# Memory attention of a streaming encoder step: heads outside, tokens inside, turned to tokens outside, heads inside

## The reference

```python
def memory_block(x, mk, mv, norm_mem_q, w_mem_q, w_mem_o):
    bsz, L, _ = x.shape
    q = (rmsnorm(x, norm_mem_q) @ w_mem_q).reshape(bsz, L, MEM_HEADS, MEM_HEAD_DIM)
    s = jnp.einsum('bqhd,bkhd->bhqk', q, mk).astype(jnp.float32) * (MEM_HEAD_DIM ** -0.5)
    p = jax.nn.softmax(s, axis=-1).astype(mv.dtype)
    o = jnp.einsum('bhqk,bkhd->bqhd', p, mv).reshape(bsz, L, D_MODEL)
    return x + o @ w_mem_o
```

## Time and profile before

| | us |
|---|---|
| median of 3 runs | 1260.66 |
| lowest, highest run | 1258.69, 1265.19 |
| the profiled execution | 1260.04 |
| its span in the profile | 1258.3 |
| TensorE busy in the span | 1157.4 (92%) |
| VectorE, ScalarE busy | 721.6 (57%), 569.8 (45%) |
| mean granted clock of TensorE | 0.955 of full speed |

### The profile page before, as it was taken

How to read it: one execution, slowest core, us unless ns; L and a number is a source line. 1 busy time by engine, 2 the same in 40 slices (tenths; PEclk the granted TensorE clock), 3 DMA queues, 4 the chain that set the end, 5 groups by cost and what they waited for, 6 DMA issues and landing times.

```text
span 1258.3 us, 18236 instructions
## 1 busy us (share of the span) xinstructions
PE 1157.4 (92%) x7804; PEld 1040.9 (83%) x7813; DVE 721.6 (57%) x844; ACT 569.8 (45%) x705; POOL 118.1 (9%) x131
## 2 busy tenths in 40 slices
PE   5998897999969999999899989879949999999996
PEld 4997676999957799999899989559938877878884
DVE  4412774565168844233334733542479998898885
ACT  4423662333147652122213612521147776877873
POOL 1000441000025300000000000000010000000032
PEclk9998788999979999999899999979969999999998
DMA  9432000222220133233425622101179999999997
GB/s 280 134 110 67 1 1 4 81 70 83 59 60 2 34 84 90 63 93 93 142 87 200 201 83 68 34 1 51 67 283 385 412 420 395 380 401 400 353 317 180
DMA packets 95005, 197.24 MB, mean 157 GB/s; under 512 B 4185, under 2 KB 71929, under 8 KB 82633
## 3 DMA queue, kind: packets, MB, share of 16 engines
q1 hardware_dynamic: 87328, 169.88, 38.4%
q0 software_dynamic: 5408, 18.76, 5.1%
q10 hardware_dynamic: 2184, 7.39, 1.4%
HBM read 178.41 MB, written 17.60 MB: 156 GB/s over the span
## 4 chain that ended last, share of the span: by engine, by line
PE 72%; DVE 12%; ACT 9%; issue 3%; DMA 3%; POOL 0%; ACTq 0%; SPq 0%; DVEq 0%; POOLq 0%
PE ps L2022 45%; PE ps L924 7%; ACT buf_r L852 3%; DVE buf_r L859 3%; PE ps L934 3%; PE ps L2389 1%; PE ps L2140 1%; DMA buf<-in_w_gate_e 1%; ACT buf_r L434 1%; PE ps L2141 1%; DVE buf_r L1060 1%; DMA buf<-in_w_in 1%; PE ps L2111 1%; ACT buf_r L422 1%; PE ps L2258 1%
## 5 line engine op out<-in xcount | busy, mean ns | idle before, releaser
L2022 PE MATMUL ps<-buf_r,buf_r 128*128 128x288 f32 (+1 forms) x4560 | 598.8, 293 | 12.8 <-DVE buf_r L438 9.7
L2022 PEld LDWEIGHTS ps<-buf_r,buf_r 128*128 128x128 f32 x4560 | 592.5, 191 | 14.7 <-issue 5.9
L428 DVE TENSOR_TENSOR buf_r<-buf,buf_r 128x2048 fp32r<-128x2048 f32 (+2 forms) x53 | 116.6, 2200 | 175.7 <-ACT buf_r L422 175.7
L859 DVE TENSOR_TENSOR buf_r<-buf,buf_r 128x2048 fp32r<-128x2048 f32 x96 | 214.1, 2284 | 3.2 <-ACT buf_r L852 3.2
L924 PE MATMUL ps<-buf_r,buf_r 128*128 128x512 f32 x768 | 186.2, 398 | 2.4 <-DVE buf_r L1060 2.4
L852 ACT CAST buf_r<-buf 128x2048 fp32r<-128x2048 f32 x96 | 178.6, 1909 | 8.1 <-DMA buf<-in_w_gate_e 6.6
L924 PEld LDWEIGHTS ps<-buf_r,buf_r 128*128 128x128 f32 x768 | 143.1, 190 | 33.2 <-DVE buf_r L1060 2.8
L422 ACT CAST buf_r<-buf 128x2048 fp32r<-128x2048 f32 (+2 forms) x53 | 96.6, 1823 | 118.0 <-PE ps L2022 65.9
L934 PE MATMUL ps<-buf_r,buf_r 128*128 128x512 f32 x384 | 91.5, 394 | 0.5 <-DVE buf_r L1092 0.5
L934 PEld LDWEIGHTS ps<-buf_r,buf_r 128*128 128x128 f32 x384 | 72.0, 188 | 17.5 <-DVE buf_r L1092 0.9
L434 ACT CAST buf_r<-ps 128x1024 fp32r<-128x1024 f32 (+1 forms) x32 | 25.6, 801 | 76.6 <-PE ps L908 62.9
(11 more groups left out here) (316 smaller groups left out, 1211.0 us busy)
## 6 DMA issues: line engine op xcount, KB each, us to landing
buf<-in_w_gate_e SPq DMA_DIRECT2D x32, 1024.0 KB, 8.0
buf<-in_w_up_e SPq DMA_DIRECT2D x32, 1024.0 KB, 8.1
buf<-in_w_down_e SPq DMA_DIRECT2D x32, 1024.0 KB, 7.2
buf<-in_w_in SPq DMA_DIRECT2D x16, 1024.0 KB, 5.7
buf<-in_w_in SPq DMA_DIRECT2D x17, 512.0 KB, 4.3
buf<-in_w_mem_kv SPq DMA_DIRECT2D x8, 1024.0 KB, 5.6
y_rows<-buf ACTq DMA_DIRECT2D x14, 512.0 KB, 8.3
buf<-in_x_prompt SPq DMA_DIRECT2D x8, 512.0 KB, 5.5
```

Source lines behind the costliest of these rows:

```text
L428: nc.vector.tensor_tensor(r32(raw), raw, w_hi(n), ALU.subtract).then_inc(wl_ready, 1)
L859: nc.vector.tensor_tensor(e_lo(t), e_raw(t), e_hi(t), ALU.subtract).then_inc(wl_ready, 1)
L2022: last = nc.tensor.matmul(out, a, b, start=(k == 0 and j == 0), stop=(k == len(parts) - 1 and j == 2))
```

## The change

The loops change places: chunk `a // 4` outside, head `a % 4` inside.

- Query half `j` is now column block `j % 8` of token half `j // 8`, so that all heads of the first two chunks can start when eight halves are done. All four query-weight tiles are held at once: high parts in `HI` and the two `HI_MO`, and the output weights take the same four buffers in turn. Halves use two banks (6 and 7) instead of four. Halves 0 and 1 stand between the key turns; steps 0 and 1 take two halves each, steps 2 to 9 one.
- The values of a step are computed one step later (`mvalues(a)`), 128 columns at a time, for two heads into one bank (4 or 5), from four small `PT` buffers. ScalarE casts the high part straight from there (`heads_high`) and VectorE subtracts from there (`heads_low`); the copy of `mem_out` and the packing of `OT_2` are gone.
- Ten of the 20 output products (chunks 0 and 1, and half of chunk 2) stand in steps 10 to 19, with their adds behind the step's scaling on VectorE. The splits of the output weights stand in steps 5, 7, 9, 11 on ScalarE and 6, 8, 10, 12 on VectorE. The other ten products follow the loop, with the router's work in a new order among them.
- The load of the gain vector and POOL's constants wait for product 10 instead of product 0. `PT` and `OT_2` have other places in memory; OT_2's no longer lies over the late buffers.

Left out of the diff are these places, renamings and unchanged lines.

```diff
-            return r32(tile_view(HI[n % NHI] if n < W_MO + 2 else HI_MO[n - W_MO - 2], n))
+            if n >= W_MQ:
+                return r32(tile_view((HI[W_MQ % NHI], HI[(W_MQ + 1) % NHI], HI_MO[0], HI_MO[1])[(n - W_MQ) % 4], n))
+            return r32(tile_view(HI[n % NHI], n))
...
         def split_high(act, n):
-            if NHI <= n < W_MO + 2:
+            if n >= W_MO:
+                act.wait_ge(*retire[n - 4])
+            elif n == W_MQ + 2:
+                act.wait_ge(tp_psum, N_G + NC_)
+            elif n == W_MQ + 3:
+                act.wait_ge(mkv_psum, 16)
+            elif n >= NHI:
...
+                                           (W_KV, 8, mkv_psum, 2), (W_MO, 4, mo_psum, NC_)):
             for j in range(count):
-                retire[first + j] = (psum, groups * (j + 1) + (Q_MEM if first == W_MQ else 0))
+                retire[first + j] = (psum, groups * (j + 1))
+        for j in range(4):
+            retire[W_MQ + j] = (q_psum, Q_MEM + KD + 2 * (j + 1))
         for c in range(KD):
             retire[W_M + 2 * c] = (gb_psum, c + 1)
...
         U_ = 10
+        STEPS = 4 * NC_
+        Q_FIRST = 4
+        Q_FILL = [(4, 5), (6, 7)] + [(j, ) for j in range(8, 16)]
+        MO_IN = 10
         OFF = [0, 512, 1024, 896]
...
-        def mem_out(act, h):
...
-                nc.scalar.copy(OT[:, 2 * h + dc, :], bank(4 + 2 * dc, 2)[:, 0:T]).then_inc(ot_ready, 1)
...
-                act_high(OTH[:, 2 * h + dc, :], OT[:, 2 * h + dc, :])
+        def heads_out(e):
...
+            m, hh = divmod(e, 2)
+            t0, n = CH[m]
+            k = slice(4 * hh, 4 * hh + 4)
+            rows = bank(4 + hh).rearrange("p (k n) -> p k n", k=4)[:, :, 0:n]
+            if m < NC_ - 1:
+                return rows, OTH[:, k, t0:t0 + n], OT[:, k, t0:t0 + n]
+            return rows, OT_2[:, k, 0:LS], OT_2[:, k, LS:2 * LS]
+        def heads_high(act, e):
+            rows, high, _ = heads_out(e)
+            act.wait_ge(ot_psum, e + 1)
+            act_high(high, rows)
+        def heads_low(dve, e):
+            rows, high, low = heads_out(e)
+            dve.wait_ge(ah_ready, A_OT + e + 1)
+            nc.vector.tensor_tensor(r32(low), rows, r32(high), ALU.subtract).then_inc(al_ready, 1)
+        def mo_bank(i):
+            return 6 + i % 2 if i < MO_IN else i % 3
+        def query_part(j):
+            return j % KD, slice((j // KD) * (T // 2), (j // KD + 1) * (T // 2))
...
-                i, h = divmod(j, 2)
...
+                i, t = query_part(j)
...
-                nc.scalar.mul(QM[:, i, h * (T // 2):(h + 1) * (T // 2)], bank(4 + j % 4)[:, 0:T // 2], MHD ** -0.5).then_inc(q_ready, 1)
-                if j % 4 == 3:
-                    split_high(act, W_MQ + 2 + j // 4)
...
+                nc.scalar.mul(QM[:, i, t], bank(6 + j % 2)[:, 0:T // 2], MHD ** -0.5).then_inc(q_ready, 1)
+            query_out(0)
+            split_high(act, W_MQ + 2)
+            query_out(1)
+            split_high(act, W_MQ + 3)
+            for j in range(2, Q_FIRST):
...
-                if a < 6:
-                    query_out(4 + 2 * a)
-                    query_out(5 + 2 * a)
-                if m == 1 and h >= 1:
-                    mem_out(act, h - 1)
-                if a in (9, 13):
-                    split_high(act, W_MO + 2 + (a > 9))
-            mem_out(act, MH - 1)
-            act.wait_ge(ah_ready, A_OT + KD)
-            nc.scalar.copy(r32(OT_2[:, :, 0:LS]), r32(OTH[:, :, LP:T])).then_inc(two_ready, 1)
+                if a < len(Q_FILL):
+                    for j in Q_FILL[a]:
+                        query_out(j)
+                if a % 2 and a >= 3:
+                    heads_high(act, (a - 3) // 2)
+                if a in (5, 7, 9, 11):
+                    split_high(act, W_MO + (a - 5) // 2)
+            heads_high(act, 2 * NC_ - 1)
...
+            split_low(dve, W_MQ + 3)
...
-                nc.vector.tensor_copy(PT[h % 2][:, :, t0:t0 + n],
+                nc.vector.tensor_copy(PT[a % 4][:, :, 0:n],
...
-            nc.vector.memset(r32(OT_END).bitcast(F32), 0.0)
-            nc.vector.memset(r32(OTH_END).bitcast(F32), 0.0)
-            def out_low(h):
-                for c in (2 * h, 2 * h + 1):
...
-            for a in range(20):
-                n = CH[a % 5][1]
-                if a in (2, 5, 7, 11, 15):
-                    split_low(dve, W_MQ + 3 + (2, 5, 7, 11, 15).index(a))
-                if a % 5 == 3 and a >= 5:
-                    out_low(a // 5 - 1)
+            def mo_add(i):
+                m, t = divmod(i, 4)
+                dve.wait_ge(mo_psum, i + 1)
+                xv = X[:CH[m][1], m, 256 * t:256 * (t + 1)]
+                if m < NC_ - 1:
+                    nc.vector.tensor_tensor(xv, xv, bank(mo_bank(i))[:, 0:256], ALU.add).then_inc(x2_ready, 1)
+                else:
+                    add_last(dve, xv, mo_bank(i), 4 + t + 1, x2_ready)
...
+            for a in range(STEPS):
+                n = CH[a // 4][1]
+                if a in (6, 8, 10, 12):
+                    split_low(dve, W_MO + (a - 6) // 2)
...
-            pt_out(19)
-            out_low(MH - 1)
-            dve.wait_ge(al_ready, A_OT + KD)
-            nc.vector.tensor_copy(r32(OT_2[:, :, LS:]), r32(OT[:, :, LP:T])).then_inc(two_ready, 1)
+                if a % 2 and a >= 3:
+                    heads_low(dve, (a - 3) // 2)
+                if a >= STEPS - MO_IN:
+                    mo_add(a - STEPS + MO_IN)
+            pt_out(STEPS - 1)
+            heads_low(dve, 2 * NC_ - 1)
...
-            for m, (_, n) in enumerate(CH):
-                for t in range(4):
-                    dve.wait_ge(mo_psum, 4 * m + t + 1)
-                    xv = X[:n, m, 256 * t:256 * (t + 1)]
-                    if m < NC_ - 1:
-                        nc.vector.tensor_tensor(xv, xv, bank((4 * m + t) % 3)[:n, 0:256], ALU.add).then_inc(x2_ready, 1)
-                    else:
-                        add_last(dve, xv, (4 * m + t) % 3, 4 + t + 1, x2_ready)
-                    if m and t == 0:
-                        ffn_scale(m - 1)
-                    if m and t == 1:
-                        ffn_gain(m - 1)
-                    if m >= 2 and t == 2:
-                        logits_out(dve, m - 2)
+            mo_add(10)
+            mo_add(11)
+            ffn_gain(0)
+            mo_add(12)
+            logits_out(dve, 0)
+            ffn_gain(1)
+            mo_add(13)
+            logits_out(dve, 1)
+            ffn_scale(0)
+            mo_add(14)
+            ffn_gain(2)
+            ffn_scale(1)
+            mo_add(15)
+            logits_out(dve, 2)
+            ffn_scale(2)
+            mo_add(16)
+            mo_add(17)
+            mo_add(18)
+            ffn_gain(3)
+            ffn_scale(3)
+            mo_add(19)
...
+            def query_half(j):
+                i, t = query_part(j)
+                if j < KD and j % 2 == 0:
+                    pe.wait_ge(wl_ready, W_MQ + j // 2 + 1)
+                if j >= 2:
+                    pe.wait_ge(q_ready, Q_MEM + j - 1)
+                n, c = W_MQ + i // 2, (i % 2) * P
+                passes(bank(6 + j % 2)[:, 0:T // 2], [((w_hi(n)[:, k, c:c + P], w_lo(n)[:, k, c:c + P]),
+                                                       (r32(HTH2[:, k, t]), r32(HT[:, k, t]))) for k in range(KD)]).then_inc(q_psum, 1)
...
+            turn_mem(0)
+            turn_mem(1)
...
-            for j in range(4):
+            query_half(0)
+            turn_mem(2)
+            query_half(1)
+            turn_mem(3)
+            for j in range(2, Q_FIRST):
...
-                h, m = divmod(a, 5)
+                m, h = divmod(a, 4)
                 t0, n = CH[m]
-                if m == 0:
-                    pe.wait_ge(q_ready, Q_MEM + 4 * (h + 1))
+                pe.wait_ge(q_ready, Q_MEM + (0 if m < 2 else KD) + 2 * (h + 1))
...
-            def mvalues(h):
-                pe.wait_ge(pt_ready, 5 * (h + 1))
+            def mvalues(a):
+                m, h = divmod(a, 4)
...
+                pe.wait_ge(pt_ready, a + 1)
+                if h % 2 == 0 and e >= 2:
+                    pe.wait_ge(al_ready, A_OT + e - 1)
                 for dc in range(2):
-                    if h >= 1:
-                        pe.wait_ge(ot_ready, 2 * (h - 1) + dc + 1)
-                    else:
-                        pe.wait_ge(q_ready, Q_MEM + 16)
                     f = h * MHD + dc * P
+                    o = ((h % 2) * 2 + dc) * P
                     for kc in range(2):
-                        nc.tensor.matmul(bank(4 + 2 * dc), MKV[:, kc, D + f:D + f + P], PT[h % 2][:, kc, 0:LP],
-                                         start=(kc == 0), stop=(kc == 1))
-                    for kc in range(2):
-                        last = nc.tensor.matmul(bank(5 + 2 * dc)[:, 0:LS], MC[:, 1, kc, f:f + P], PT[h % 2][:, kc, LP:T],
+                        vv = MKV[:, kc, D + f:D + f + P] if m < 4 else MC[:, 1, kc, f:f + P]
```

(58 more changed lines are left out.)

45 lines of the change are left out of this document (14 added, 31 removed).

## The result

| | before | after |
|---|---|---|
| median (lowest, highest), us | 1262.04 (1258.69, 1265.19), 5 runs | 1253.16 (1249.29, 1254.24), 5 runs |
| ratio to before, 95% interval | | 0.9934 (0.9908 to 0.9960) |
| the profiled execution, its span | 1260.04, 1258.3 | 1253.16, 1251.3 |
| first key turn | 722.67 | 723.45 |
| end of product 19 | 908.04 | 896.02 |

The account below looks back on a forecast made before the run. TensorE bounds the kernel, with waits in the first and third of four stretches. Stretches of 16.7, 112.5 and 37.7 us end product 19 at 889.6, 18.4 us earlier, giving a median of 1242.3 us, range 1237 to 1251.

Parts of the forecast that it names:

- First stretch: From the first key turn to the first scores: 16.7 us instead of 22.3, a gain of 5.6 us.
- Waits in the loop: TensorE's waits in the softmax loop: 5.9 us, from 1.7, 1.7 and 2.1 at steps 6, 8, 10 and 0.4 elsewhere.
- the third scores: In the softmax loop, TensorE's third scores wait for query copy 5, some 0.4 us.
- More waiting: Rival: in the loop's last ten steps queueing eats the slack and adds 1 us each, giving 1252 us; chance 0.11.
- less waiting: Rival: the three split waits and the router wait are hidden, 8 us less, 1234 us; half of them, 1238; chance 0.09.
- Work in the loop: TensorE's work in the softmax loop, from query halves, scores, transposes, output products and values: 106.6 us without waits.
- the weight loads show: Rival: in the loop's values no weight load is hidden, costing 16 us, so 1258 us, the same; chance 0.02.
- Third stretch: From the loop's end to the end of product 19: 37.7 us instead of 64.1.
- the router scores' wait: Before product 19, chunk 3's router scores wait 2.5 us for VectorE's HT copy, behind product 18's adds.
- the rival for the loop: TensorE drops to 1.2 GHz for long; all ten last steps at that level make 1290 us; chance 0.04.
- Nothing is lost downstream: Behind product 19 the expert phase shifts as a block, so the whole 18.4 us gain arrives at the end.
- The rival of a loss downstream: An expert-phase event, a store or POOL's first gather, does not move with product 19: 1260 us, the same; chance 0.03.

Follow-up runs that it names:

- split_early: Changed kernel with ScalarE's high split of an output-weight tile ahead of the query copy and heads' cast of its step: 1245.91 us, ratio 0.9895 to the kernel before.
- gain_early: Changed kernel with VectorE's copy of the turned rows of chunk 3 ahead of product 18's adds: 1243.60 us, ratio 0.9879 to the kernel before.
- keep_busy: Changed kernel with 20 unread transposes on TensorE between product 18 and the router scores of chunk 3: 1240.77 us, ratio 0.9858 to the kernel before.
- the two shifts: Unread transposes heading TensorE's program: 104 in the kernel before (1261.94 us, late gap of 3.6 us), 32 in the changed kernel (1246.42 us, no gap).

## Where the prediction was right, and where it was wrong

*First stretch: right.* 16.9 us against 16.7. The gain of some 5.5 us included slow clock (0.92 in the earlier trace rows) that I had put down to copies.

*Waits in the loop: right in place and cause, 0.9 us too long in all.* 1.5, 1.5 and 1.8 us at steps 6, 8 and 10 against 1.7, 1.7 and 2.1, and 0.3 at the third scores; none at 12 or in any ordinary step. split_early confirms the cause, ScalarE's order, for 3.6 of these 4.7 us. "More waiting" and "less waiting" both fell.

*Work in the loop: 3.1 us too little* (109.7 = 114.7 - 5.0 of waits, against 106.6). The waits, forecast 0.9 too long, hid part of this, so the loop came out only 2.2 off, which is luck. The values of a prompt chunk are 0.89 us a step, as taken, so "the weight loads show" fell with them. The terms that were sized too small are those beside the sample chunk, whose tiles are 64 wide. Its values take 0.97 to 1.03 a step instead of 0.78, and the last values of a prompt chunk, which stand behind 64-wide transposes, 1.09 instead of 0.87: 1.1 us in all. The four products that follow its scores take 3.06 to 3.07 instead of 2.87, 0.8 us. The trace of before had shown this last cost, at the sample chunk's first scores and the two query halves behind them, which elsewhere take 0.87 and 6.40:

```profile
768.55 1.01 PE ps L2376 x4
769.56 6.59 PE ps L2022 x48
```

I had counted it for the scores and not for the pieces behind them. And a piece behind a wait restarts slowly: the transposes 0.44 instead of 0.22, three times, and the third scores 1.13 instead of 0.87, 0.9 us in all. The values of the prompt chunks, 0.89 instead of 0.87, make the last 0.3.

*Third stretch: the wait was right, its price was not.* I wrote 2.5 us for the router scores' wait and it took 2.3. The step that failed is that I charged a wait with its own length alone and put the slow clock behind it at nothing. I had taken from the earlier trace rows that the clock falls behind waits, had put that into the rival for the loop, and had left it out of the one place to which the change adds a wait: 3.3 us more, as gain_early and keep_busy show.

*"Nothing is lost downstream": wrong, by a cause that no view of before showed.* From product 19 to the first tokens it is 22.5 us, as foreseen (22.2), and the experts are a block. But the hole in the spread and what follows it cost 4.8 us (24.5 against 19.7), 4.7 of it up to the end. The rival of a loss downstream named a store or POOL's gather; it was the place of the code, shown by the two shifts.

In sum, at the spans: 18.4 forecast, 7.0 measured. Of the 11.4 between them 5.6 lie before the end of product 19, 4.7 behind the first expert tokens, 0.3 between product 19 and the first tokens, and 0.8 in the first 723 us, which the change doesn't touch. keep_busy loses the slow clock and the hole, while the time of the wait stays, filled with transposes. Its ratio is 0.9858 (0.9822 to 0.9893), where the forecast's was 0.9854. That agrees within the noise, and in part by luck: product 19 ends 169.5 us behind the first key turn in it, not 166.9, because the loop's work is still larger than forecast.

## What to carry to other kernels

A wait that a change adds on TensorE can cost twice: its length, and the work behind it at half clock. Here a wait of 2.3 us cost 5.6, and 2.2 us of useless transposes in its place won 3 back. When an interleaving works, look for the odd steps (here those with a split, on an engine whose order puts a copy and a cast ahead of it), since ordinary steps cover each other. And compare the far end of the program too: code that is longer or shorter can open or close a hole there. If the trace gives such a hole to nothing and a packet of the instruction queue lies in it, some unread instructions at the head of the program tell whether the place of the code is its cause.
